# MLP up projection by quarter products in seven of eight iterations, with prepared activations fetched from memory in turn

## The chip, the cores and the metric

The kernel runs on one core of one Trainium2 chip. The metric is the device time of one execution in microseconds (us). The engines are named as in the profile: PE multiplies matrices (PEld is its weight load), DVE does elementwise work, ACT evaluates and copies, POOL issues part of the transfers, SP issues the others.

## The reference

One layer of a streaming encoder on x (1 x 1024 x 1024, f32): normalisation, three token-mixing branches, an output projection with a residual, and then the MLP, which is the part that is changed.

```python
x = x + rmsnorm(merged @ w_out[l], g_mix_post[l])
h = rmsnorm(x, g_mlp_pre[l])
f = jnp.square(jax.nn.relu(h @ w_up[l])) @ w_down[l]   # w_up 1024 x 4096, w_down 4096 x 1024
x = x + rmsnorm(f, g_mlp_post[l])
```

## The kernel before

Every f32 operand of a large product is held as a high part (hi: the value rounded by a copy on ACT) and a low part (lo: value minus hi, a subtraction on DVE). One product of a 128-deep slice is three matmuls of 128x512: hi by hi, hi by lo, lo by hi. `hThi`/`hTlo` hold the transposed MLP input h (8 slices k of 128 by 1024 tokens), `whi`/`wlo` and `raw` two slots (UP0, UP1) of 2048 columns of weights each, `yhi`/`ylo` the squared activations f, `acc` the output sum, and eight PSUM banks of 128x512, numbered by events n (bank n % 8), or taken as four pairs of 128x1024.

The MLP runs in eight iterations over 512 of the 4096 hidden units. In each, the up projection is eight pieces of 8 x 3 matmuls (192). The down projection of iterations 0 to 6 is already done by quarters: by the Strassen-Winograd scheme a 2 x 2 block product takes seven quarter products (`PRODUCTS`, 7 x 24 = 168 matmuls) instead of eight. DVE makes sums of quarters of f (`f_quad`) and differences of quarters of the weights (`w_diff`), ACT and DVE split them, and DVE adds finished pairs of banks to quarters of `acc` (`add_pair`, line 1621). The last iteration takes its down projection plainly (16 pieces of 12, 192 matmuls), because the final normalisation follows tile by tile.

Each engine works through a list written out by hand (in `mlp` of its block) and waits on semaphores. `w_hi`/`w_lo` count split weights, `f_sq`/`f_hi`/`f_lo` the activations, `pair_full`/`pair_free` the pairs of banks. SP loads a slot of `raw` (1 MB in two pieces of 512 KB) once the count of `w_lo` says that it has been read. A loop body covers iterations 1 to 6.

Of the kernel before, what the change touches and what calls it, by code (L numbers as in the profile page):

```python
# [16 lines left out]
P = 128  # L17
D = 1024
L = 1024
KT = D // P  # L20
NT = L // P
# [5 lines left out]
BT = W512 // P  # L27
# [95 lines left out]
PRODUCTS = [("A11", 0, 0), ("A12", 1, 1), ("S1", 2, 2), ("S2", 3, 3), ("S4", 0, 0), ("S3", 1, 2), ("A22", 2, 3)]  # L123


SET_A, SET_B = ("A11", "S2", "S3", "A22"), ("A12", "S1", "S4")
# [22 lines left out]
def hybrid_layer(nc, a, out):  # L149
# [4 lines left out]
    with ctx:  # L154
# [153 lines left out]
        sums_made, diffs_made, joined = sem("sums_made"), sem("diffs_made"), sem("joined")  # L308
        pair_full = [sem(f"pair_full{k}") for k in range(4)]
        pair_free = [sem(f"pair_free{k}") for k in range(4)]  # L310
        x1_back = [sem(f"x1_back{s}") for s in range(3)]
# [47 lines left out]
        W0 = U_MLP - U_QX  # L359
        UP0, UP1 = U_MLP % 2, 1 - U_MLP % 2  # L360
        RAW_D0, RAW_D1 = UP1, UP0
# [6 lines left out]
        def raw_half(slot, k):  # L368
# [3 lines left out]
        w_diff = {"T1": raw_half(RAW_D0, 0), "T2": raw_half(RAW_D0, 0), "B22": raw_half(RAW_D1, 1), "T3": raw_half(RAW_D1, 0),  # L372
                  "T4": raw_half(RAW_D0, 1)}
        w_place = {"T1": (UP1, 0), "T2": (UP1, 1), "B22": (UP0, 0), "T3": (UP1, 0), "T4": (UP1, 1)}
# [5 lines left out]
        def part_of(w, name):  # L380

            slot, k = w_place[name]
            return w[:, slot, 1024 * k:1024 * k + 1024]

        def pair_index(name, h):

            return h if name in SET_A else 2 + h

        def tiles_of(name):

            return (2, 3, 0, 1) if name == "A11" else range(4)

        def pair_count(name):

            return 1 + (SET_A if name in SET_A else SET_B).index(name)

        def pair_per(name):

            return 4 if name in SET_A else 3

        def wait_pair(eng, sems, name, h, it, done=0):

            count = pair_count(name) - 1 + done
            eng.wait_ge(sems[pair_index(name, h)], count + it * pair_per(name))

        def wait_pair_full(eng, name, h, it):
            wait_pair(eng, pair_full, name, h, it, 1)

        def f_place(s, c, h):

            return f_quad[("A11", "A12", "A21", "A22")[2 * h + s]][:, c, :]
# [7 lines left out]
        def _(sp):  # L419
# [65 lines left out]
            with sp.Fori(0, 8) as it:  # L485
                for s, count in ((0, W0 - 1), (1, W0)):
                    pieces = cols(U_MLP + s, up[:, bass.ds(it * 512 + s * 256, 256)])
                    sp.wait_ge(w_lo, count + it * 8)
                    for dst, src in pieces:
                        sp.dma_start(dst, src).then_inc(w_loaded[(U_MLP + s) % 2], 16)  # L490
                for s, slot, count in ((0, RAW_D0, W0 + 2), (1, RAW_D1, W0 + 1)):
                    pieces = cols(slot, down[bass.ds(it * 512, 512), s * 512:(s + 1) * 512], BT)
                    sp.wait_ge(w_lo, count + it * 8)
                    for dst, src in pieces:
                        sp.dma_start(dst, src).then_inc(w_loaded[slot], 16)
            rows = out[0].rearrange("(c i) d -> i c d", i=STEP)
            for t in range(NT):
                sp.wait_ge(out_made, t + 1)
                if t < NT - 1:
                    sp.dma_start(rows[t], tok[:, (1 + t % 3) * D:(2 + t % 3) * D]).then_inc(out_sent[t % 3], 16)  # L500
            c = (1 + (NT - 1) % 3) * D
            sp.dma_start(rows[NT - 1, :, 0:512], tok[:, c:c + 512]).then_inc(out_sent[1], 16)
            sp.wait_ge(out_made, NT + 1)
            sp.dma_start(rows[NT - 1, :, 512:D], tok[:, c + 512:c + D]).then_inc(out_sent[1], 16)
# [5 lines left out]
        def _(pool):  # L510
# [133 lines left out]
            pool.wait_ge(joined, 3)  # L644
            g.dma_start(tok[:, 0:D], a["g_mlp_post"][0].partition_broadcast(P)).then_inc(last_gain, 16)

            def x1_load(t):
                g.dma_start(tok[:, (1 + t % 3) * D:(2 + t % 3) * D], x1_dram[t * P:(t + 1) * P, :]).then_inc(x1_back[t % 3], 16)

            for t in range(3):  # L650
                x1_load(t)
# [6 lines left out]
        def _(act):  # L658
# [299 lines left out]
            def weight_hi(count, it, dst, source, load_of):  # L958

                act.wait_ge(*load_of)  # L960
                A.activation(dst, source, ACT.Copy).then_inc(w_hi, 1)  # L961

            def first_hi(it):
                wait_pair_full(act, "S4", 1, it)
                weight_hi(9, it, whi[:, UP0, :], raw[:, UP0, :], loaded(UP0, U_MLP, it + 1))

            def second_hi(it):
                wait_pair_full(act, "A22", 1, it - 1)
                weight_hi(2, it, whi[:, UP1, :], raw[:, UP1, :], loaded(UP1, U_MLP + 1, it))

            def third_hi(it):
                weight_hi(3, it, whi[:, UP0, :], raw[:, RAW_D0, :], loaded(RAW_D0, U_MLP + 3, it))

            def up_pieces(it, first):
                for pc, (s, c, h) in enumerate(UP_FIRST if first else UP_LATER):
                    n = up_event(pc, first)
                    if first and pc in (2, 3):
                        h2_hi(pc + 4)
                    if pc == (6 if first else 4):
                        wait_full(act, n - 1, it, 8)  # L980
                        third_hi(it)
                    if first and pc == 0:
                        act.wait_ge(sq_o, NT)
                        act.wait_ge(sq_x, NT)
                        act.wait_ge(x1_made, NT)
                    if first and pc == 2:
                        act.wait_ge(h2_made, NT)
                    if first and pc == 4:
                        act.wait_ge(x1_sent, 16 * NT)
                    wait_full(act, n, it, 8)  # L990
                    A.activation(f_place(s, c, h), banks[n % 8][:, :], ACT.Relu).then_inc(bank_free[n % 8], 1)  # L991
                    if h == 0:
                        act.wait_ge(f_sq, it * 8 + pc + 1)
                        A.activation(y_place(yhi, s)[:, c, :], f_place(s, c, h), ACT.Copy).then_inc(f_hi, 1)

            def f_hi_of(name, q, made, it):
                act.wait_ge(sums_made, it * 4 + made)
                A.activation(y_place(yhi, q), f_quad[name], ACT.Copy).then_inc(f_hi, 1)

            def w_hi_of(name, made, it):  # L1000
                if made:
                    act.wait_ge(diffs_made, it * 4 + made)
                A.activation(part_of(whi, name), w_diff[name], ACT.Copy).then_inc(w_hi, 1)

            def mlp(it, first):
                if not first:
                    second_hi(it)
# [1180 lines left out]
```

## Time and profile before

| what | us |
|---|---|
| median of 3 runs | 1515.39 (1513.56 to 1515.7) |
| profiled execution, its own time | 1513.69 |
| its span, first to last instruction | 1511.9 |
| PE busy | 1493.2 |
| DVE busy | 969.6 |
| ACT busy | 495.0 |
| POOL busy | 117.6 |

The span is that of one profiled execution; its own time lies 1.8 us above it. Busy time of PE counts overlapped matmuls once. A busy share says little by itself of what a change in one stage is worth; the chain that ended last does.

### The profile page before, as it was taken

The numbers are of one execution on the slowest core, as the hardware profiler recorded it, in microseconds if no ns is written. First come the engines' busy times: TensorE is split into PE (matmuls) and PEld (weight loads), VectorE is DVE, ScalarE is ACT, GpSimd is POOL, SyncE is SP. The second block draws the span as 40 slices with busy tenths as digits, with TensorE's granted clock in tenths as the row PEclk, the third lists the DMA queues.
The fourth block names the chain that finished last, engine by engine and source line by source line (L and its number), as shares of the span: only waits on it lengthen the run. The fifth ranks groups of instructions, "written<-read, shape, count | busy, mean of one in ns | idle before, by whom it ended". The sixth has DMA issues, their size and how long they took to land.

```text
span 1511.9 us, 18643 instructions
## 1 busy us (share of the span) xinstructions
PE 1493.2 (99%) x7366; PEld 1241.6 (82%) x7366; DVE 969.6 (64%) x1646; ACT 495.0 (33%) x670; POOL 117.6 (8%) x184
## 2 busy tenths in 40 slices
PE   8999999999999999999999999999999999999997
PEld 7888788888888888888888888888888888888886
DVE  6768568665844734446856776674839384856748
ACT  4435753322222352211334432222323232323232
POOL 0000000140220221000000200000000000000000
PEclk9999999999999999999999999999999999999999
DMA  8301121232112256324343303030211111020314
GB/s 320 71 28 56 63 78 38 102 112 105 64 64 100 61 165 205 104 86 152 131 126 106 98 1 111 0 112 0 67 44 55 55 55 55 28 83 1 110 56 181
DMA packets 82098, 130.44 MB, mean 86 GB/s; under 512 B 13128, under 2 KB 55152, under 8 KB 82032
## 3 DMA queue, kind: packets, MB, share of 16 engines
q1 hardware_dynamic: 67552, 80.23, 16.1%
q0 software_dynamic: 14480, 49.32, 9.6%
q8 instruction: 44, 0.72, 0.2%
q14 instruction: 22, 0.18, 0.0%
HBM read 104.36 MB, written 25.17 MB: 86 GB/s over the span
## 4 chain that ended last, share of the span: by engine, by line
PE 95%; DVE 4%; issue 0%; DMA 0%; ACT 0%; DVEq 0%; ACTq 0%; POOLq 0%
PE bank L1745 69%; PE bank L2140 18%; PE bank L1755 3%; PE bank L1785 1%; PE bank L1992 1%; PE bank L1878 1%; DVE tok L1714 1%; PE bank L2007 1%; PE bank L2012 1%; PE bank L1976 1%; PE bank L1893 0%; PE bank L1948 0%; DVE acc L1722 0%; DVE prob L1213 0%; DVE yst L1727 0%
## 5 line engine op out<-in xcount | busy, mean ns | idle before, releaser
L1745 PE MATMUL bank<-hThi,whi 128*128 128x512 f32 x1184 | 463.1, 391 | 0.5 <-DVE prob L1213 0.4
L1745 PE MATMUL bank<-hThi,wlo 128*128 128x512 f32 x1184 | 460.8, 389 | 0.0
L1745 PE MATMUL bank<-hTlo,whi 128*128 128x512 f32 x1184 | 460.8, 389 | 0.0
L1745 PEld LDWEIGHTS bank<-hThi,whi 128*128 128x128 f32 x1184 | 222.2, 188 | 47.9 <-issue 1.8
L1745 PEld LDWEIGHTS bank<-hThi,wlo 128*128 128x128 f32 x1184 | 222.3, 188 | 46.3
L1745 PEld LDWEIGHTS bank<-hTlo,whi 128*128 128x128 f32 x1184 | 222.3, 188 | 45.6
L2140 PE MATMUL bank<-whi,yhi 128*128 128x512 f32 x392 | 152.5, 389 | 0.0
L2140 PE MATMUL bank<-whi,ylo 128*128 128x512 f32 x392 | 152.5, 389 | 0.0
L2140 PE MATMUL bank<-wlo,yhi 128*128 128x512 f32 x392 | 152.5, 389 | 0.0
L1621 DVE TENSOR_TENSOR acc<-bank,acc 128x1024 f32<-128x1024 f32 x84 | 100.0, 1218 | 24.3 <-PE bank L2140 24.3
L1572 DVE TENSOR_TENSOR wlo<-raw,whi 128x1024 fp32r<-128x1024 f32 (+1 forms) x58 | 95.0, 1639 | 2.2 <-ACT whi L961 2.2
L345 ACT ACTIVATE whi<-raw 128x2048 fp32r<-128x2048 f32 x30 | 57.4, 1918 | 104.0 <-PE bank L1745 70.1
L351 DVE TENSOR_TENSOR wlo<-raw,whi 128x2048 fp32r<-128x2048 f32 x31 | 70.9, 2290 | 29.5 <-ACT whi L345 29.0
L2140 PEld LDWEIGHTS bank<-whi,ylo 128*128 128x128 f32 x392 | 73.6, 188 | 15.3
L2140 PEld LDWEIGHTS bank<-whi,yhi 128*128 128x128 f32 x392 | 73.6, 188 | 15.3
L2140 PEld LDWEIGHTS bank<-wlo,yhi 128*128 128x128 f32 x392 | 73.6, 188 | 15.3
L790 ACT ACTIVATE scr<-bank 128x512 f32<-128x512 f32 x48 | 28.5, 598 | 159.5 <-PE bank L1745 150.6
L1599 DVE TENSOR_TENSOR yst<-yst 128x512 f32<-128x512 f32 x28 | 19.4, 692 | 94.6 <-ACT yst L991 94.6
L961 ACT ACTIVATE whi<-raw 128x2048 fp32r<-128x2048 f32 x23 | 44.1, 1916 | 88.8 <-PE bank L2140 88.8
L1599 DVE TENSOR_TENSOR tok<-tok 128x512 f32<-128x512 f32 x28 | 19.3, 691 | 60.7 <-ACT tok L991 60.7
L991 ACT ACTIVATE yst<-bank 128x512 f32<-128x512 f32 x28 | 16.7, 598 | 115.7 <-PE bank L1745 115.7
L1448 DVE TENSOR_TENSOR tok<-bank,tok 128x512 f32<-128x512 f32 x8 | 5.5, 691 | 69.9 <-PE bank L2012 69.4
(361 smaller groups left out, 2192.3 us busy)
## 6 DMA issues: line engine op xcount, KB each, us to landing
raw<-in_w_in_dram SPq DMA_DIRECT2D x34, 512.0 KB, 4.6
raw<-in_w_up_dram SPq DMA_DIRECT2D x32, 512.0 KB, 4.3
raw<-in_w_down_dram SPq DMA_DIRECT2D x32, 512.0 KB, 5.1
gate_scratch<-scr POOLq DMA_DIRECT2D x48, 256.0 KB, 2.3
tok<-gate_scratch POOLq DMA_DIRECT2D x24, 512.0 KB, 3.6
y_scratch<-yst POOLq DMA_DIRECT2D x16, 256.0 KB, 2.5
yst<-y_scratch POOLq DMA_DIRECT2D x16, 256.0 KB, 4.1
raw<-in_w_out_dram SPq DMA_DIRECT2D x8, 512.0 KB, 4.3
```

Source lines behind the costliest of these rows:

```text
L345: nc.scalar.activation(parts(u)[0], raw[:, u % 2, :], ACT.Copy).then_inc(w_hi, 1)
L351: nc.vector.tensor_tensor(lo, raw[:, u % 2, :], hi.bitcast(f32), sub).then_inc(w_lo, 1)
L790: A.activation(scr[:, gp % 2, :], banks[n % 8][:, :], ACT.Sigmoid).then_inc(bank_free[n % 8], 1)
L961: A.activation(dst, source, ACT.Copy).then_inc(w_hi, 1)
L991: A.activation(f_place(s, c, h), banks[n % 8][:, :], ACT.Relu).then_inc(bank_free[n % 8], 1)
L1572: V.tensor_tensor(lo, source, hi.bitcast(f32), sub).then_inc(w_lo, 1)
L1599: V.tensor_tensor(f, f, f, mul).then_inc(f_sq, 1)
L1621: V.tensor_tensor(dst[:, 2 * h:2 * h + 2, :], psum[:, 2 * k:2 * k + 2, :], dst[:, 2 * h:2 * h + 2, :], add).then_inc(pair_free[k], 1)
L1714: V.scalar_tensor_tensor(out=xt[:, h], in0=yx[:, t % 2, h], scalar=y[:, k:k + 1], in1=xt[:, h], op0=mul, op1=add)\
L1745: ins = T.matmul(dst, lhs(k)[p], rhs(k)[q], start=start and k == 0 and i == 0, stop=stop and k == kt - 1 and i == 2)
L1755: ins = T.transpose(banks[n % 8][:, i * P:i * P + P] if dsts is None else dsts[i], src, by)
L2140: ins = T.matmul(banks[2 * k + t % 2][:, :], x[:, kk, rows], w[:, kk, :], start=opens and kk == 0 and i == 0, stop=kk == 1 and i == 2, ski ...
```

## The change

The up projection is done by seven quarter products as well, in iterations 1 to 7 (`up_phase(m)`, m = 0 to 6); the down projection stays at seven products in iterations 1 to 6 (`down_phase(m)`) and is plain in the first and in the last. The first iteration is plain in both parts (`plain_mlp`): 192 + 192 matmuls.

The up products need four combinations of quarters of h (T1 to T4). They are computed once, in the first iteration, by eight calls of `step(i)` on DVE (two halves of four sums), split by ACT (`step_high`) and DVE into the one buffer `staged` and stored by POOL to `h_scratch`; the plain quarter B11 is stored as well. T3 replaces a quarter of `hThi`/`hTlo` for good. T2 is fetched to the free half of `yhi`/`ylo` in each iteration; T1, T4 and B11 take turns in one quarter of `hThi`/`hTlo` (`turn_load`), fetched by POOL in two parts of 2 x 512 KB. A part is fetched when the half product that read it is done.

A repetition of the new loop body has on DVE 56 operations of 128x1024, on ACT 24, on PE 14 products of 24 matmuls: uP1, uP2, uP6, uP5, uP7, uP3, uP4, then dP1, dP5, dP6, dP3, dP7, dP2, dP4. There are 14 weight parts j = 0 to 13 (`W_PARTS`), each split by `w_hi_of(j)` and `w_lo_of(j)`.

```diff
+UP_PRODUCTS = [("uP1", 0, 0), ("uP2", 1, 1), ("uP6", 3, 2), ("uP5", 2, 3), ("uP7", 4, 0), ("uP3", 5, 1), ("uP4", 6, 2)]
+DOWN_PRODUCTS = [("dP1", 0, 1, 3), ("dP5", 2, 2, 0), ("dP6", 3, 3, 1), ("dP3", 0, 5, 2), ("dP7", 2, 6, 0), ("dP2", 1, 4, 1), ("dP4", 0, 7, 2)]
...
 SP
+            def mlp(m, last):
+                units = [down_unit(0, m + 1), down_unit(1, m + 1)]
+                if not last:
+                    units += [up_unit(0, m + 2), up_unit(1, m + 2)]
+                unit_load(UP0, units[0], w_count(5, m))
+                unit_load(UP1, units[1], w_count(6, m))
+                if not last:
+                    unit_load(UP1, units[3], w_count(11, m))
+                    unit_load(UP0, units[2], w_count(13, m))
...
 POOL
+            def turn_load(which, name, use, m):
+                pool.wait_ge(turn_used, use + 3 * m)
+                h_back(which, 0, turn, turn_in)
+                pair_ready(pool, name, m)
+                h_back(which, 1, turn, turn_in)
...
+            for i in range(8):
+                pool.wait_ge(step_lo, i + 1)
+                for hl in range(2):
+                    g.dma_start(h_dram[STEP_ORDER[i % 4], hl, :, 2 * (i // 4):2 * (i // 4) + 2, :], staged[hl]).then_inc(step_out, 16)
...
+            def streams(m, last):
+                turn_load(S_T1, "uP1", 1, m)
+                turn_load(S_T4, "uP5", 2, m)
+                if last:
+                    return
+                turn_load(S_B11, "uP4", 3, m)
+                pair_ready(pool, "dP2", m)
+                for k in range(2):
+                    h_back(S_T2, k, kept2, kept_in)
...
 ACT
+            def step_high(i):
+                act.wait_ge(step_made, i + 1)
+                if i:
+                    act.wait_ge(step_out, 32 * i)
+                A.activation(staged[0], step_sum(i), ACT.Copy).then_inc(step_hi, 1)
...
+                f_hi_of("A22", 0)
+                diff(8, m)
+                w_hi_of(13, m)
+                next_units(m + 1, [lambda: pair_ready(act, "dP7", m), lambda: pair_ready(act, "dP2", m), lambda: None])
...
 DVE
+            def step(i):
...
+                if i:
+                    dve.wait_ge(step_out, 32 * i)
+                dve.wait_ge(step_hi, i + 1)
+                V.tensor_tensor(staged[1], step_sum(i), staged[0].bitcast(f32), sub).then_inc(step_lo, 1)
...
+                    if pc == 6:
+                        prep_lo(dve, U_MLP + 2)
...
+                    if pc >= 4:
+                        step(pc - 4)
+                prep_lo(dve, U_MLP + 3)
+                for s in range(2):
+                    for t in range(NT):
...
+                        V.tensor_tensor(acc[:, t, h], banks[n % 8][:, :], acc[:, t, h], add).then_inc(bank_free[n % 8], 1)
+                        if t % 4 == 1:
+                            step(4 + 2 * s + t // 4)
+                        if s and t == 5:
+                            next_first(0)
+                for n in range(F + 16, F + 24):
+                    wait_taken(dve, n)
+                for k in range(4):
+                    dve.sem_inc(pair_free[k], 1)
...
+            def middle_quad(name, out_of, other, m):
+                pair_ready(dve, out_of, m)
+                k, q = pair_of(out_of, 1), f_quad[name]
+                V.tensor_tensor(q, pair_banks(k), f_quad[other], add).then_inc(pair_free[k], 1)
+                pair_read(dve, out_of, m)
+                V.scalar_tensor_tensor(out=q, in0=q, scalar=0.0, in1=q, op0=ALU.max, op1=mul).then_inc(f_sq, 1)
...
+                w_lo_of(6, m)
+                pair_read(dve, "uP6", m)
+                pair_read(dve, "uP5", m)
+                V.tensor_tensor(f_quad["A22"], f_quad["A22"], f_quad["A12"], add).then_inc(common_made, 1)
...
+                if last:
+                    join(2)
...
+                    dve.wait_ge(w_hi, w_count(7, m))
+                    V.tensor_tensor(wlo[:, UP0, :], raw[:, UP0, :], whi[:, UP0, :].bitcast(f32), sub).then_inc(w_lo, 1)
+                    middle_quad("A21", "uP3", "A12", m)
+                    f_lo_of("A21", 2, 3, m)
...
+                    return
+                w_lo_of(7, m)
+                dve.wait_ge(w_lo, w_count(7, m))
+                dve.wait_ge(*loaded(UP1, U_MLP + 3, m + 1))
+                w_diff(raw_half(UP0, 0), raw_half(UP1, 0), raw_half(UP0, 0), 5, m)
+                w_diff(raw_half(UP1, 0), raw_half(UP1, 1), raw_half(UP1, 0), 6, m)
+                dve.wait_ge(common_made, 1 + m)
+                middle_quad("A22", "uP7", "A22", m)
+                w_lo_of(8, m)
+                dve.wait_ge(w_lo, w_count(8, m))
+                w_diff(raw_half(UP0, 0), raw_half(UP1, 1), raw_half(UP0, 0), 7, m)
+                middle_quad("A21", "uP3", "A12", m)
+                w_lo_of(9, m)
+                squared(3, m)
+                dve.wait_ge(f_lo, 8 + 1 + 7 * m)
+                V.tensor_tensor(f_quad["S3"], f_quad["A11"], f_quad["A21"], sub).then_inc(sums_made, 1)
+                dve.wait_ge(sums_made, 1 + 4 * m)
+                V.tensor_tensor(f_quad["S1"], f_quad["A21"], f_quad["A22"], add).then_inc(sums_made, 1)
+                V.tensor_tensor(f_quad["S2"], f_quad["A22"], f_quad["S3"], sub).then_inc(sums_made, 1)
+                middle_quad("A12", "uP4", "A12", m)
+
+            def down_phase(m, first=False):
+                f_lo_of("S1", 2, 2, m)
...
+                f_lo_of("A22", 0, 7, m)
+                w_lo_of(13, m)
+                add_pair("dP7", 0, c22, m, "dP5")
+                add_pair("dP7", 1, c22, m, "dP5")
+                add_pair("dP2", 0, c11, m, "dP1")
+                w_lo_of(0, m + 1)
+                add_pair("dP2", 1, c11, m, "dP1")
+                dve.wait_ge(w_lo, w_count(0, m + 1))
+                dve.wait_ge(*loaded(UP1, U_MLP + 1, m + 2))
+                w_diff(raw_half(UP0, 0), raw_half(UP0, 0), raw_half(UP1, 0), 1, m + 1)
+                add_pair("dP4", 0, c21, m)
+                next_second(m + 1, lambda: add_pair("dP4", 1, c21, m))
...
 PE
-            mlp(0, True)
-            with pe.Fori(1, 7) as it:
-                mlp(it, False)
-            up_pieces(7, False)
+            plain_mlp()
+            with pe.Fori(0, 6) as m:
+                up_phase(m)
+                down_phase(m)
+            up_phase(6)
```

The last down projection and the final normalisation take the row tiles in the order 4 to 7, 0 to 3 (`tile_of`); the three sums of `common` into `acc` (2048 columns each) stand between DVE's operations of the last up phase.

## Rows read from the trace of the kernel before

**Rows 1.** The page: span, and busy time of the two busiest engines.

```profile
span 1511.9 us, 18643 instructions
...
PE 1493.2 (99%) x7366; PEld 1241.6 (82%) x7366; DVE 969.6 (64%) x1646; ACT 495.0 (33%) x670; POOL 117.6 (8%) x184
```

**Rows 2.** The chain that ended last, in order of time: start, us, what.

```profile
887.34 38.08 PE bank L2140 x168
...
1333.42 43.52 PE bank L1745 x192
1376.94 38.08 PE bank L2140 x168
1415.02 57.13 PE bank L1745 x252
1472.17 0.70 DVE acc L1722
```

**Rows 3.** Busy time by engine in one steady iteration: span, busy (count), clock, DMA.

```profile
1007.00:1089.00 82.00, 82.00 (x364) 67.89 (x363) 52.23 (x48) 23.28 (x26) 0.00 (x0) 1.00 0.15 51
```

**Rows 4.** Groups by line and shape in the MLP, 900 to 1490 us.

```profile
L1621 DVE TENSOR_TENSOR acc<-bank,acc 128x1024 f32<-128x1024 f32 x82 | 97.7, 1218 | 24.0 <-PE bank L2140 24.0
...
L1572 DVE TENSOR_TENSOR wlo<-raw,whi 128x2048 fp32r<-128x2048 f32 x22 | 50.2, 2282 | 2.2 <-ACT whi L961 2.2
L961 ACT ACTIVATE whi<-raw 128x2048 fp32r<-128x2048 f32 x22 | 42.1, 1916 | 88.8 <-PE bank L2140 88.8
L1572 DVE TENSOR_TENSOR wlo<-raw,whi 128x1024 fp32r<-128x1024 f32 x33 | 40.1, 1216 | 0.0
L1003 ACT ACTIVATE whi<-raw 128x1024 fp32r<-128x1024 f32 x32 | 33.1, 1054 | 35.3 <-DVE raw L1658 21.3 <-DVE raw L1638 14.0
...
L994 ACT ACTIVATE yhi<-tok 128x512 fp32r<-128x512 f32 x24 | 15.2, 633 | 18.2 <-DVE tok L1599 18.2
```

**Rows 5.** Timeline of DVE in a steady iteration: start, us, what, idle before.

```profile
1018.57 0.69 DVE L1599 TENSOR_TENSOR tok<-tok 128x512 f32<-128x512 f32 x1 [3.36 <-ACT tok L991]
1019.96 0.69 DVE L1603 TENSOR_TENSOR ylo<-tok,yhi 128x512 fp32r<-128x512 f32 x1 [0.70 <-ACT yhi L994]
...
1046.38 1.22 DVE L1613 TENSOR_TENSOR raw<-raw 128x1024 f32<-128x1024 f32 x1
1047.63 1.23 DVE L1615 TENSOR_TENSOR raw<-raw 128x1024 f32<-128x1024 f32 x1
...
1054.21 1.22 DVE L1572 TENSOR_TENSOR wlo<-raw,whi 128x1024 fp32r<-128x1024 f32 x1
1055.35 1.22 DVE L1588 TENSOR_TENSOR ylo<-yst,yhi 128x1024 fp32r<-128x1024 f32 x1
...
1069.48 1.22 DVE L1572 TENSOR_TENSOR wlo<-raw,whi 128x1024 fp32r<-128x1024 f32 x1
```

**Rows 6.** Timeline of SP: weight loads of one iteration, four pieces in each row.

```profile
1011.77 2.10 SPq L495 DMA_DIRECT2D raw<-in_w_down_dram  x4
1070.86 8.86 SPq L490 DMA_DIRECT2D raw<-in_w_up_dram  x4
```

**Rows 7.** Landing of `raw` pieces issued 1070 to 1073, 1012.4 to 1014, 845 to 860 us.

```profile
DMA to landing us min/median/max: 3.6/4.0/4.4
...
DMA to landing us min/median/max: 4.4/5.6/6.3
...
DMA to landing us min/median/max: 7.9/7.9/7.9
```

**Rows 8.** Landing of single 512 KB stores by POOL, issued at 773.8 and 847.3 us.

```profile
x_scratch<-yst POOLq DMA_DIRECT2D x1, 512.0 KB, 2.9
...
x_scratch<-yst POOLq DMA_DIRECT2D x1, 512.0 KB, 6.6
```

**Rows 9.** Landing of one load in the crowded first 60 us of the kernel.

```profile
vT<-in_w_mem_kv_dram SPq DMA_DIRECT2D x1, 512.0 KB, 10.6
```

**Rows 10.** Timeline of ACT: fifth up piece of the first iteration.

```profile
871.12 0.60 ACT L991 ACTIVATE yst<-bank 128x512 f32<-128x512 f32 x1 [3.51 <-PE bank L1745]
```

More of the change, by code:

```diff
@@ L385, in pair_index @@
[L385 to L404, printed above, removed]
@@ new lines, in plain_mlp @@
+                for i, (t, s) in enumerate((t, s) for s in range(2) for t in range(NT)):
+                    n = F + 8 + i
+                    if t == 0:
+                        unit(U_MLP + 2 + s)
+                    hi, lo = wviews(U_MLP + 2 + s, BT)
+                    wait_free(pe, n)
+                    if s == 0 and t in (0, 4):
+                        pe.wait_ge(f_lo, 6 if t == 0 else 8)
+                    product(banks[n % 8][:, :], yT(slice(t * P, t * P + P)), lambda k: (hi[:, k, :], lo[:, k, :]), BT)\
+                        .then_inc(bank_full[n % 8], 1)
@@ new lines, in up_phase @@
+            def up_phase(m):
+                turn, kept3 = ([h_quarter(y, 0, t) for y in (hThi, hTlo)] for t in range(2))
+                b21, b22 = ([h_quarter(y, 1, t) for y in (hThi, hTlo)] for t in range(2))
+                kept2 = [second_half(y) for y in (yhi, ylo)]
+                moving = {"uP1": turn, "uP2": b21, "uP6": kept2, "uP5": turn, "uP7": kept3, "uP3": b22, "uP4": turn}
+                for name, j, place in UP_PRODUCTS:
+                    k = pair_of(name, 1)
+                    pe.wait_ge(w_lo, w_count(j, m))
+                    pe.wait_ge(pair_free[k], pair_before(k, name, m))
+                    hi, lo = (w_slot(w, place).rearrange("p (k c) -> p k c", k=4) for w in (whi, wlo))
+                    h, opens = moving[name], name not in ("uP6", "uP3", "uP4")
+                    use = ("uP1", "uP5", "uP4").index(name) if h is turn else None
+                    for part in range(2):
+                        if h is turn:
+                            pe.wait_ge(turn_in[part], 32 * (1 + use) + 96 * m)
+                        if h is kept2:
+                            pe.wait_ge(kept_in[part], 32 + 32 * m)
+                        for c in range(2):
+                            for kk in (2 * part, 2 * part + 1):
+                                for i, (w, x) in enumerate(((hi, h[0]), (hi, h[1]), (lo, h[0]))):
+                                    ins = T.matmul(banks[2 * k + c][:, :], w[:, kk, c * P:c * P + P], x[:, kk, :], start=opens and kk == 0 and i == 0,
+                                                   stop=kk == 3 and i == 2, skip_group_check=True)
+                        if part:
+                            ins.then_inc(pair_full[k], 1)
+                        elif h is turn:
+                            ins.then_inc(turn_used, 1)
```

563 lines of the change are left out of this document (327 added, 236 removed).

## The prediction

> **What bounds the kernel now.** I read the page first: PE is busy for 1493.2 of 1511.9 us, DVE for 969.6 [rows 1]. A busy share is no proof, so the chain that ended last came next. Through the MLP it holds only PE: up projections of 43.52 us for 192 matmuls and down projections of 38.08 us for 168 follow each other without a gap, and the last 252 matmuls take 57.13 us. All give 0.2267 us a matmul [rows 2]. DVE enters the chain only at 1472.17 us, for the final normalisation. Then the stretch of one steady iteration (81.6 us, read over 82): PE is busy throughout at a granted clock of 1.00 (the 2.4 GHz level), DVE for 52.2 us, ACT for 23.3, the DMA engines for 0.15 of it [rows 3]. So taking matmuls away is worth their whole time until another queue is late.
>
> The profiled execution took 1513.69 us by its own time, 1.7 below the median of the runs; I subtract from 1513.69 and add 1.7 at the end.
>
> **Matmuls.** Before: 7 x (192 + 168) + 192 + 192 = 2904 of 512 columns. After: 384 in the first iteration, 6 x 336, and 168 + 192 in the last, 2760. So 144 go: 144 x 0.2267 = 32.6 us. They have the shape of the others. A product is 24 matmuls, 5.44 us; a repetition of the loop is 76.16 us if PE never waits.
>
> **Prices of the walk.** I walk through the lists. DVE: an operation of 1024 columns lasts 1.22 us [rows 4], the next one starts 1.13 after it, or 1.25 if it waits for its result [rows 5]. The new operation (maximum and product in one) is not in these rows; between 1.13 and the 1.25 of a dependent one, I take 1.25, as it does depend. ACT: 1.05 us for 1024 columns, 1.92 for 2048 [rows 4]. A handover between engines is about 0.03 us: DVE idles 0.70 around a copy of 0.633 [rows 4, 5]. A weight slot has landed 5.1 us after the `w_lo` that releases it: that operation ends at 1070.70, SP issues at 1070.86 and 0.57 later, the second piece lands 4.4 us on [rows 5 to 7].
>
> **DVE is nearly full.** 56 operations of 1.13 us are 63.5 of 76.16 us, and some wait. With t = 0 where uP1 starts, the products end at 5.44, 10.88, 16.32 (uP6), 21.76 (uP5), 27.20 (uP7), 32.64 (uP3), 38.08 (uP4), and each down product 5.44 later. Up to uP5 DVE waits for PE (its operation on uP2 starts at 10.93). Then:
> - ACT takes uP5's banks, 21.8 to 22.84. DVE: common sum 22.87, w_lo 7 at 24.0, w_diff 5 at 25.25 at best, since it waits for w_lo 7 and for a weight slot.
> - w_diff 6 26.5, two operations on uP7 27.6 and 28.9, w_lo 8 30.0, w_diff 7 31.3, and then uP3, ready at 32.69: a slack of 0.3.
> - From there nine operations back to back (uP3 twice, w_lo 9, S3, S1, S2, uP4 twice, f_lo S1) end at 43.34. dP5 starts at 43.52 and needs S1: a slack of 0.15.
> - In the down phase 20 operations run to w_lo 13, which ends at 65.1. That releases slot UP0, landed at 70.2; ACT's w_hi 0, w_lo 0 at 71.3, the add of dP2, w_diff 1, the first add of dP4, which ends at 75.95. It frees the pair that uP1 needs at 76.16: a slack of 0.2.
> - The split of weights for uP2 ends 2.1 us into the next repetition, for uP6 at 8.4, each ahead of use.
>
> PE is therefore kept busy by a chain of DVE with about 0.4 us of slack over 54 us. What makes w_diff 5 late makes dP5 late, and every repetition longer.
>
> **The fetch that is late.** w_diff 5 needs slot UP1, released by w_lo 6 at 19.61. Alone it lands at 24.7, in time. But POOL starts on T4 at 19.04 (half of uP5 is done): two pieces at once, two more at 21.76. Four pieces issued within 2.1 us have all landed 1.7 + 6.3 = 8.0 us after the first issue [rows 6, 7]: 19.1 + 8.0 = 27.1. A store that joins four loads 2.5 us later moves the last load from 6.3 to 7.9 us [rows 7] and itself takes 6.6 instead of 2.9 [rows 8], so the two pieces at 21.76 can add 1.6: 28.7. I take 27.5, nearer the first, since of the four pieces the slot's two were issued last but share the engines with the other queue. Its cost: 27.53 - 25.25 - 0.42 of slack = 1.8 us a repetition, 10.8 in six. Bounds: 0, if the slot lands as alone, and 5.3 (31.6 in all), if its second piece takes the 10.6 us of the crowded start [rows 9] from 20.3 on.
>
> The Trainium skill (DMA: Bandwidth & Descriptors, Anatomy of one DMA) fits a transfer as 2.0 us plus its bytes at 436 GB/s. For the four pieces (2.1 MB) that is an estimate of 6.8 us against the 8.0 of the row; the slot would be there at 25.9 and the cost 0.3 a repetition, 1.6 in all. The row decides. The same page (Queues, rings and completion order) says that a DMA engine takes the queues that have work in turn, which would let T4 halve the slot's rate; no row separates this.
>
> The other fetches of a repetition are costed at nothing. T1 has from 2.7 and 5.4 to 16.3; T4 is issued by 22.3 and needed from 32.6; B11 and T2 are issued 40 and 16 us ahead. They would cost what they are late. 12.6 MB in 76 us are 165 GB/s, where 51 take a share of 0.15 [rows 3], so the engines are half used. ACT's 24 operations (25 us) hide as long as none is last in a handover; where one is, it stands in the walk.
>
> **The first iteration** gets its 24 matmuls more (counted), and DVE 26 more operations: eight steps of three or four. `staged` is one buffer, so lo of a step comes after the stores of the step before: handover, two stores, ACT's hi, DVE's lo. Two stores together are not shown; one alone lands in 2.9 us, one beside four loads in 6.6 [rows 8], a pair of loads in 5.1; I take 5.1. From the fifth piece, whose copy starts at 871.12 [rows 10]: lo of step 0 ends at 879.7, stores landed 884.8, hi and lo of step 1 end at 887.15. ACT starts on the first down weights behind that hi, at 885.8, DVE splits them at 887.8, done 890.1, where PE is ready at 887.34 [rows 2]: 2.8 us idle. Behind DVE now queue adds to `acc` and PE's banks. The steps go on at 7.4 to 10 us each (lo ends at 896.8, 904.3, 914.3, 921.7, 929.2, 937.2). PE's 16 down tiles (2.72 us each, 43.5) end at 933.7, but uP1 waits for the last add, behind step 7, w_lo 0 and w_diff 1: 940.9. 7.2 us idle. With stores of 2.9 this falls to about 7.5 in all, with 6.6 it is 17.5.
>
> **The last iteration.** DVE splits 2048 columns of w_down only when uP3 has released them (ACT 32.7 to 34.6, DVE to 36.9), then takes uP3 (38.1, 39.3), ACT's hi to 40.4, lo to 41.7. The plain down projection needs that quarter at 38.08: 3.6 us idle. Of two bounds (0 by PE, 3.6 by the walk) I take the walk. The final part is the same work behind PE; its start moves with PE, and the adds that wait (DVE is free 5.7 us after the down start) are caught up before 13.6, where its chain begins.
>
> **Sum.** 32.6 - 2.8 - 7.2 - 3.6 - 10.8 = 8.2 us. 1513.69 - 8.2 = 1505.5; on the scale of the runs 1507.2.
>
> **Rivals.**
> - The slot is hidden: T4's first pieces are ahead and the slot lands by 25.7. 19.0 us gained, 1496.4. For: the engines are used at 0.15 now, and POOL's 0.7 us lead. Against: [rows 7, 8] show five pieces slowing each other. Chance 0.25.
> - Slower: the loads meet as in the first 60 us, the slot lands at 30.9, 5.3 us a repetition: 19.0 - 31.6 = -12.6, 1528.0. It decides from 3.2 us a repetition, a landing at 28.9. Against: the five pieces of [rows 7, 8] have none above 7.9. Chance 0.13.
> - The stores cost 6.6 us: the first iteration idles 17.5 instead of 10, gain 0.7, 1514.7, no change. For: some of the eight pairs meet weight loads and the fetch of T3. Against: most are alone. Chance 0.12.
> - The forecast, stores near 5 us and a stall of 0.5 to 2.6 at dP5: 0.45, its own range 1502 to 1514. The rest, 0.05, is an order that I walked wrongly.
>
> A run of this kernel tells about 0.2% (3.0 us) from no change: 1512.4 to 1518.4. Faster: 0.45 + 0.25 and 0.02 of the others, 0.72; same 0.12; slower 0.16. The range reaches from the hidden slot (1496) to part of the slower case: 1495 to 1520.
>
> **What would show it.** The stretch of a repetition: 76.2 us (hidden), 78 (forecast), over 79.4 (slower); DVE busy about 64 of it; PE idle at dP5 with DVE's f_lo of S1 as releaser, and DVE idle ahead of w_diff 5 with a DMA into `raw`. PE idle 2.8 us ahead of the first down tile, 7 ahead of uP1, 3.6 ahead of the last down part. Idle at uP5 or uP4 itself would mean that the turned quarters are late, and idle at uP1 that slot UP0 is; both would make the prediction wrong by a place that I price at nothing.

## The result, and the profile after

The changed kernel takes 1528.44 us (median of 4, 1525.75 to 1530.46), the kernel before 1515.4 in the same comparison: ratio 1.0087, 95% interval 1.0070 to 1.0105. It is slower by 13 us. The forecast was 1507.2 with a range up to 1520, so the sign and the range were both wrong. Its own forecast for a single profiled execution was 1505.5; that execution took 1530.46, 25.0 us more. These 25.0 us are what has to be explained.

The page of the changed kernel, its span and the busy time of the engines:

```profile
span 1528.7 us, 18594 instructions
...
PE 1478.7 (97%) x7222; PEld 1224.8 (80%) x7222; DVE 1072.6 (70%) x1721; ACT 507.2 (33%) x663; POOL 202.1 (13%) x314
```

Beside [rows 1]: 144 matmuls fewer, as planned, but PE's busy time fell by only 14.5 us where 144 matmuls are 32.6. The rest of those 32.6 came back as busy time, which points to slower matmuls; the windows below show where. DVE has 103 us more.

The chain that ended last, in order of time (start, duration, what), for the first iteration, one repetition of the loop that starts at 1110.31, the two after it, and the last iteration:

```profile
924.74 5.38 DMA h_scratch<-tok
...
933.44 6.13 DMA h_scratch<-tok
...
945.95 18.99 PE bank L2372 x72
...
1110.31 16.33 PE bank L2372 x72
...
1128.67 1.24 DVE wlo L1768
...
1130.33 7.93 DMA raw<-in_w_down_dram
1138.37 1.24 DVE raw L1778
...
1155.11 1.23 DVE ylo L1772
1156.55 35.78 PE bank L2392 x144
1192.33 16.34 PE bank L2372 x72
...
1238.56 32.94 PE bank L2392 x144
1271.51 16.34 PE bank L2372 x72
...
1431.67 32.65 PE bank L2372 x144
...
1473.53 15.35 PE bank L1968 x60
```

Where [rows 2] had nothing but PE, the chain now leaves PE in every repetition, after the first half of the up phase: a split of weights on DVE (1128.67), the load of a down weight slot (7.93 us), `w_diff 5` (1138.37), DVE's list up to the low part of S1 (1155.11), and then PE's down phase. Two more things are to be read here. The 144 matmuls behind `dP5` take 35.78 us in one repetition and 32.94 in another: the same instructions, so the clock differs. And uP1 of the first repetition begins at 945.95, behind stores of the prepared sums.

PE's waits from 860 to 1480 us (place, what ended them: sum, count, longest, in us):

```profile
PE bank L2392 <- DVE ylo L1772: 16.6, 6, 3.0
...
PE bank L2372 <- DVEq L1761: 8.6, 1, 8.6
...
PE bank L1968 <- DVE ylo L1772: 3.8, 1, 3.8
PE bank L1968 <- DVE wlo L364: 2.2, 1, 2.2
```

They are the four places of the forecast, in the order of these lines: dP5 in each of six repetitions (2.77 us each, forecast 1.8), uP1 of the loop (8.6, forecast 7.2), the last down part (3.8, forecast 3.6), the first down tile (2.2, forecast 2.8). Their sum is 31.2 where the forecast had 24.4. That explains 6.8 us of 25.0.

The windows of three repetitions, and of 2 us steps behind the idle time of the second, then the first 4 us of the loop and the first 6 us of the last down part (stretch, length, busy of PE, PEld, DVE, ACT, POOL, granted clock, DMA share, GB/s):

```profile
1029.70:1110.30 80.60, 78.08 (x337) 64.12 (x337) 65.49 (x57) 24.52 (x25) 10.61 (x16) 0.98 0.52 156
1110.30:1192.30 82.00, 79.28 (x338) 65.03 (x337) 65.55 (x57) 24.62 (x25) 10.60 (x16) 0.96 0.50 153
1192.30:1271.50 79.20, 76.48 (x338) 63.00 (x337) 64.40 (x56) 24.22 (x24) 10.59 (x16) 1.00 0.52 160
...
1154.30:1156.30 2.00, 0.00 (x0) 0.00 (x0) 2.00 (x3) 1.59 (x2) 0.00 (x0) 0.87 0.06 18
1156.30:1158.30 2.00, 1.75 (x4) 1.47 (x5) 2.00 (x3) 0.00 (x0) 0.00 (x0) 0.50 0.00 0
1158.30:1160.30 2.00, 2.00 (x6) 1.52 (x6) 2.00 (x3) 0.00 (x0) 0.00 (x0) 0.50 0.00 0
1160.30:1162.30 2.00, 2.00 (x7) 1.52 (x6) 2.00 (x3) 0.00 (x0) 0.00 (x0) 0.50 0.00 0
1162.30:1164.30 2.00, 2.00 (x10) 1.62 (x9) 2.00 (x3) 1.07 (x1) 0.00 (x0) 0.92 0.00 0
...
946.00:950.00 4.00, 4.00 (x10) 3.13 (x11) 3.69 (x4) 1.06 (x1) 3.40 (x5) 0.50 0.08 19
...
1474.00:1480.00 6.00, 6.00 (x22) 4.74 (x22) 5.93 (x6) 1.31 (x2) 0.53 (x1) 0.78 0.01 3
```

Beside [rows 3]: the clock column is no longer 1.00 throughout. Behind the idle time that ends at 1156.55 the granted clock stands at 0.50 (the 1.2 GHz level) for 6 us, with PE busy in every one of them. A repetition of 79.2 us kept its clock; the others paid for it. DVE is busy for 64.4 to 65.5 us, where the forecast said about 64.

The slot that is late: landing of the `raw` pieces issued from 1110 to 1133 us (against [rows 7]), and DVE's timeline in the same repetition:

```profile
DMA to landing us min/median/max: 3.8/4.6/7.9
```

```profile
1134.38 1.22 DVE L1768 TENSOR_TENSOR wlo<-raw,whi 128x1024 fp32r<-128x1024 f32 x1
1138.37 1.23 DVE L1778 TENSOR_TENSOR raw<-raw 128x1024 f32<-128x1024 f32 x1 [2.77 <-DMA raw<-in_w_down_dram]
```

DVE stands still for 2.77 us ahead of `w_diff 5` for a piece that needs 7.9 us. The window of that landing shows what the share of 0.50 for the whole repetition hides:

```profile
1129.90:1138.30 8.40, 8.40 (x39) 6.96 (x38) 2.36 (x2) 1.98 (x2) 2.58 (x4) 1.00 0.93 283
```

The DMA engines are 0.93 busy while the slot is on its way (0.60 in the 5.2 us in which the same slot lands when T4 is held back). The prediction's "the engines are half used" was an average over 76 us. Placed on the forecast's own clock (t = 0 at uP1, 1110.31): w_lo 6 ends at 19.59 (forecast 19.61), the slot has landed at 27.96 (forecast 27.5), w_diff 5 starts at 28.06 (27.53), dP5 at 46.24 where 43.52 would be without a wait.

### The profile page after: what moved, and what is told of

It is laid out like the page before. It is cut to its first block, busy times and chain, and to the rows that moved or that the text cites. A ratio compares the mean times of both kernels' runs of the same rounds, so it can differ in the third digit from the quotient of the medians.

```text
span 1528.7 us, 18594 instructions
## 1 busy us (share of the span) xinstructions
PE 1478.7 (97%) x7222; PEld 1224.8 (80%) x7222; DVE 1072.6 (70%) x1721; ACT 507.2 (33%) x663; POOL 202.1 (13%) x314
## 4 chain that ended last, share of the span: by engine, by line
PE 78%; DVE 11%; DMA 5%; issue 4%; ACT 2%; POOL 0%; DVEq 0%; SPq 0%; ACTq 0%; POOLq 0%
PE bank L1968 47%; PE bank L2392 13%; PE bank L2372 9%; DMA raw<-in_w_down_dram 3%; PE bank L1978 3%; PE bank L2008 2%; DMA h_scratch<-tok 1%; DVE wlo L1768 1%; DVE yst L1809 1%; PE bank L2215 1%; PE bank L2101 1%; DVE tok L1936 1%; DVE raw L1778 1%; DVE ylo L1772 1%; PE bank L2230 1%
## 5 line engine op out<-in xcount | busy, mean ns | idle before, releaser
L1968 PE MATMUL bank<-hThi,whi 128*128 128x512 f32 x736 | 288.8, 392 | 0.5 <-DVE prob L1350 0.4
L1968 PE MATMUL bank<-hThi,wlo 128*128 128x512 f32 x736 | 286.5, 389 | 0.0
L1968 PE MATMUL bank<-hTlo,whi 128*128 128x512 f32 x736 | 286.5, 389 | 0.0
L1079 ACT ACTIVATE whi<-raw 128x1024 fp32r<-128x1024 f32 x91 | 95.9, 1056 | 207.1 <-DVE raw L1778 119.8
L1968 PEld LDWEIGHTS bank<-hThi,whi 128*128 128x128 f32 x736 | 138.2, 188 | 30.5 <-issue 1.8
L1968 PEld LDWEIGHTS bank<-hThi,wlo 128*128 128x128 f32 x736 | 138.1, 188 | 28.9
L1968 PEld LDWEIGHTS bank<-hTlo,whi 128*128 128x128 f32 x736 | 138.2, 188 | 28.1
L2392 PE MATMUL bank<-whi,yhi 128*128 128x512 f32 x336 | 134.5, 400 | 16.6 <-DVE ylo L1772 16.6
L2372 PE MATMUL bank<-hThi,whi 128*128 128x512 f32 x336 | 131.8, 392 | 8.6 <-DVEq L1761 8.6
L2372 PE MATMUL bank<-hTlo,whi 128*128 128x512 f32 x336 | 131.7, 392 | 0.0
L2372 PE MATMUL bank<-hThi,wlo 128*128 128x512 f32 x336 | 131.5, 391 | 0.0
L1768 DVE TENSOR_TENSOR wlo<-raw,whi 128x1024 fp32r<-128x1024 f32 x91 | 110.9, 1219 | 29.2 <-ACT whi L1079 29.1
L358 ACT ACTIVATE whi<-raw 128x2048 fp32r<-128x2048 f32 x32 | 61.2, 1916 | 104.2 <-PE bank L1968 70.2
L2392 PEld LDWEIGHTS bank<-whi,yhi 128*128 128x128 f32 x336 | 64.9, 193 | 32.9 <-issue 19.1
L2372 PEld LDWEIGHTS bank<-hThi,whi 128*128 128x128 f32 x336 | 63.7, 190 | 22.3 <-issue 9.0
L1778 DVE TENSOR_TENSOR raw<-raw 128x1024 f32<-128x1024 f32 x52 | 63.6, 1222 | 20.0 <-DMA raw<-in_w_down_dram 16.9
```

Of the source, the lines that this page charges most:

```text
L358: nc.scalar.activation(parts(u)[0], raw[:, u % 2, :], ACT.Copy).then_inc(w_hi, 1)
L1079: A.activation(w_slot(whi, place), source, ACT.Copy).then_inc(w_hi, 1)
L1768: V.tensor_tensor(w_slot(wlo, place), source, w_slot(whi, place).bitcast(f32), sub).then_inc(w_lo, 1)
L1778: V.tensor_tensor(dst, x, y, sub if count != 2 else add).then_inc(diffs_made, 1)
L1968: ins = T.matmul(dst, lhs(k)[p], rhs(k)[q], start=start and k == 0 and i == 0, stop=stop and k == kt - 1 and i == 2)
L2372: ins = T.matmul(banks[2 * k + c][:, :], w[:, kk, c * P:c * P + P], x[:, kk, :], start=opens and kk == 0 and i == 0, stop=kk == 3 and i == ...
```

## Where the 25.0 us are

| place | forecast | measured | difference |
|---|---|---|---|
| all up to 870 us, unchanged code | 0 | later by 2.4 | 2.4 |
| first iteration, up to uP1 of the loop | uP1 at 940.9 | 943.6 (945.95 less the 2.4) | 2.7 |
| loop: idle ahead of dP5, six times | 10.8 | 16.6 | 5.8 |
| loop: low clock behind idle time | 0 | 10.4 | 10.4 |
| loop: small pauses | 0 | 0.3 a repetition | 1.8 |
| last iteration, 1431.67 to the end | 95.0 | 97.0 | 2.0 |

The differences add up to 25.1; the rest is rounding. The clock's 10.4 are read from equal pieces of work: the six groups of 144 matmuls take 34.56, 34.57, 35.78, 32.94, 32.95 and 34.54 us, 7.7 more than six times 32.94; the first 72 matmuls of the loop take 18.99 instead of 16.33, 2.7 more.

The first line is not the change's doing. One group of 16 matmuls of the memory projection starts at about the same time in both executions and takes longer in one. The chain of the kernel before and, under it, of the changed one:

```profile
10.87 3.69 PE bank L1785 x16
```

```profile
10.92 6.06 PE bank L2008 x16
```

Everything up to 870 us is shifted by those 2.4 us. Between 12 and 14 us PE does 6 matmuls in the second and 11 in the first, though the clock column shows 1.00 in both; why is open. The group takes 3.69 us in eight of the profiled executions of this record, 6.06 in two and 5.36 in one, so two medians that lie some 2 us apart can differ by this alone.

## The experiments

All of them start from the changed kernel. Those with a filler add matmuls that nothing reads; nothing is left out in any. Two readings of the loop stood against each other. One: POOL's fetch of T4 is ahead of the weight slot in the DMA engines, this makes `w_diff 5` and so dP5 late, and the low clock is what follows from PE's pause. The other: DVE's list is too full, or the slot is slow by itself, and the clock falls for a reason of its own.

**T4 behind the slot.** POOL waits until slot UP1 has landed before it fetches T4.

```diff
+                pool.wait_ge(*loaded(UP1, U_MLP + 3, m + 1))
                 turn_load(S_T4, "uP5", 2, m)
```

> POOL starts the fetch of T4 only when the weight slot that w_diff 5 waits for has landed. Theory (the two loads meet on the DMA engines, the slot lands 8.3 us after its release instead of 5.1, PE idles about 3 us at dP5 and the granted clock then falls for some us): no idle at dP5 beyond 0.3 us, a repetition takes 76.2 to 76.8 us instead of 80.95 on average, and the time is 1528.4 - 6 x 4.45 = 1501.7 us (1499 to 1505). Rival (DVE's 56 operations and their handovers are too long by themselves, the slot is only the last of several): a repetition stays at 79 us or more and the time above 1518.

Measured: 1506.68 us (1502.64 to 1507.6), ratio 0.9949 (0.9932 to 0.9966), against 1515.13 for the kernel before. It is 21.8 us less than the changed kernel, and faster than the kernel before. The median is 1.7 us above the expected interval; the profiled execution (1502.64) is the fastest of the four. Landing of the slot pieces of a repetition, the chain for a repetition, its window, PE's waits and DVE's timeline around `w_diff 5`:

```profile
DMA to landing us min/median/max: 3.6/4.1/4.7
```

```profile
1022.20 38.08 PE bank L2373 x168
...
1065.89 32.95 PE bank L2393 x144
```

```profile
1022.20:1098.80 76.60, 76.42 (x337) 62.95 (x337) 64.94 (x57) 24.36 (x24) 10.59 (x16) 1.00 0.55 164
```

```profile
PE bank L2373 <- DVEq L1762: 8.6, 1, 8.6
...
PE bank L2393 <- DVE ylo L1773: 0.7, 4, 0.2
```

```profile
1122.91 1.22 DVE L1769 TENSOR_TENSOR wlo<-raw,whi 128x1024 fp32r<-128x1024 f32 x1
1124.36 2.49 DVE L1779 TENSOR_TENSOR raw<-raw 128x1024 f32<-128x1024 f32 x2 [0.24 <-DVE wlo L1769]
```

The last piece needs 4.7 us instead of 7.9, DVE's pause of 2.77 is gone, PE waits 0.7 us at dP5 in four repetitions together, the clock is 1.00, and the repetition takes 76.6 us, where 76.16 is what its matmuls need. DVE's busy time is the same, 64.9 us: the list was not too full. T4 itself, fetched later, is waited for once, 0.4 us in the last iteration. One wait on POOL takes away the idle time and the low clock of the loop together: it takes 462.2 us (943.18 to 1405.37) instead of 485.7. The pause ahead of the last down part is 3.1 us long here, and the clock stays at 1.00 behind it.

**A filler in PE's pause.** Twelve matmuls that nothing reads fill most of the pause ahead of dP5. The pause stays, so the difference is the clock alone.

```diff
             def down_phase(m):
                 for p, (name, q, parts_made, place) in enumerate(DOWN_PRODUCTS):
+                    if name == "dP5":
+                        pe.wait_ge(pair_free[2], pair_before(2, name, m))
+                        filler(banks[4], 12)   # matmul(banks[4], hThi[:, 4, 512:640], hThi[:, 4, 512:1024])
                     pe.wait_ge(f_lo,
```

> PE runs 12 matmuls of 128x512 whose result nobody reads (2.7 us, into a bank that dP5 opens anew) ahead of its wait at dP5; everything else is as changed. Theory (half the loss over the wait itself is the clock that falls after the idle time): the granted clock stays at 1.00 and all six repetitions take 79.0 to 79.5 us, as the two that kept their clock; 1528.4 - 6 x 1.75 = 1518 us (1515 to 1521). Rival (the low clock has another cause, or the filler delays dP5): 1526 or more.

Measured: 1521.43 us (1519.34 to 1522.82), ratio 1.0045 (1.0029 to 1.0062). The chain of one repetition and its window:

```profile
1104.91 38.08 PE bank L2372 x168
...
1151.28 32.89 PE bank L2399 x144
```

```profile
1104.90:1184.20 79.30, 79.17 (x350) 65.28 (x349) 65.13 (x57) 24.36 (x24) 10.60 (x16) 1.00 0.52 158
```

The clock stays at 1.00 at dP5. Five repetitions take 79.0 to 79.3 us, where the changed kernel had 79.2 to 82.0; the first still takes 82.0 (83.7), since the low clock at uP1 isn't touched by this edit, and there "all six" was a miss. DVE's lateness is untouched. The loop takes 477.8 us instead of 485.7, the median is 7.0 lower: that was the clock behind the pauses at dP5, and it goes with the pauses. The clock has no reason of its own. The time is 0.4 us above the expected interval; the length of a repetition is as expected.

**Order in the last iteration.** DVE takes uP3's products ahead of the split of 2048 columns of weights.

```diff
+                    middle_quad("A21", "uP3", "A12", m)
                     dve.wait_ge(w_hi, w_count(7, m))
                     V.tensor_tensor(wlo[:, UP0, :], raw[:, UP0, :], whi[:, UP0, :].bitcast(f32), sub).then_inc(w_lo, 1)
-                    middle_quad("A21", "uP3", "A12", m)
```

> In the last up phase DVE takes uP3's pair before it splits the 2048 columns of w_down. Theory (the last down projection waits 3.8 us for the low part of that quarter, and then runs some us at the low clock): its start moves 3.2 us earlier and the clock stays, 1528.4 - 4.6 = 1524 us (1522.5 to 1526). Rival (the final DVE chain sets the end, so an earlier start of PE is lost in it): 1527.5 or more.

Measured: 1522.17 us (1520.84 to 1522.59), ratio 1.0050 (1.0033 to 1.0067), 6.3 us less than the changed kernel. PE's wait ahead of the last down part is down from 3.8 us to 0.6. The place was read rightly. The median is 0.3 us below the expected interval, and part of the 6.3 us isn't this edit's: in its profiled execution the untouched loop takes 483.2 us instead of 485.7, since fewer repetitions fell to the low clock.

**Only T4's second half behind the slot.** POOL's two first pieces go as in the changed kernel, and the two others wait. This asks which pieces hold the slot up.

```diff
                 h_back(which, 0, turn, turn_in)
                 pair_ready(pool, name, m)
+                if name == "uP5":
+                    pool.wait_ge(*loaded(UP1, U_MLP + 3, m + 1))
                 h_back(which, 1, turn, turn_in)
```

> Only the second half of T4 waits until the weight slot has landed; the first half still starts with it. Theory A (the two pieces issued later take engine time from the slot, the term that the prediction halved): the slot lands at 27.1 us of a repetition or before instead of 27.96, w_diff 5 starts 0.9 us or more earlier, a repetition takes 77.8 to 78.4 us where the clock stays at 1.00 (79.2 as changed), time 1519 to 1523. Theory B (only what is queued ahead of the slot delays it): landing at 27.9 and no change, 1527 to 1530.

Measured: 1523.07 us (1519.72 to 1524.19), ratio 1.0063 (1.0045 to 1.0081). The time alone would speak for a gain of 5.4 us. The rows don't: landing of the slot's pieces in the repetition that starts at 1105.03, DVE's timeline there, and PE's waits:

```profile
DMA to landing us min/median/max: 3.7/4.6/7.8
```

```profile
1132.99 2.48 DVE L1780 TENSOR_TENSOR raw<-raw 128x1024 f32<-128x1024 f32 x2 [2.67 <-DMA raw<-in_w_down_dram]
```

```profile
PE bank L2394 <- DVE ylo L1774: 14.9, 6, 2.6
```

The last piece lands after 7.8 us, not 7.9; `w_diff 5` starts at 1132.99 - 1105.03 = 27.96 of the repetition, not 28.06; the wait at dP5 is 2.5 us, not 2.8. This is the slowest of the six: in their mean DVE idles 2.5 us ahead of `w_diff 5`, where it is 2.8 in the changed kernel and 0.2 with all of T4 behind the slot. So it is T4's first two pieces that delay it (in the changed kernel's repetition at 1110.31 they are issued at 1129.67 and 1130.36, the slot's last piece at 1130.33), and the two issued 2.4 and 3.1 us after the slot's last piece cost 0.3 us a repetition. Of the 5.4 us, 1.7 are those waits. The rest is covered by the clock, which fell in two repetitions of this execution and in four of the other (34.52, 32.93, 34.54, 32.95, 32.95, 32.93 us for 144 matmuls: 3.2 us instead of 7.7). Which repetitions fall isn't set by the code alone.

**Order at the end of the first iteration.** Step 7 of the preparation moves behind the last adds and the weights for the loop, on DVE and ACT; POOL fetches T2 and T1 for the first repetition ahead of the last two stores.

```diff
 DVE
-                        if t % 4 == 1:
+                        if t % 4 == 1 and not (s and t == 5):
                             step(4 + 2 * s + t // 4)
...
                 next_second(0)
+                step(7)
 POOL
-            for i in range(8):
+            for i in range(7):
                 sum_out(i)
...
+            pool.wait_ge(step_out, 32 * 7)
+            turn_load(S_T1, "uP1", 1, 0)
+            sum_out(7)
```

> In the first iteration the last of the eight sums is made, split and stored after the last adds into acc and after the first weight splits of the loop, and the fetches of T2 and T1 go ahead of its stores. Theory (the steps' wait for stores holds the adds that free PE's banks): PE idles 1 to 3 us ahead of uP1 instead of 8.6, uP1 starts some 5 us earlier, and the low clock behind it shrinks; 1528.4 - 6 = 1522.5 us (1520 to 1525). Rival (the delay only moves into uP6 or uP5, whose operands come later): 1527 or more, with PE idle at one of these.

Measured: 1518.21 us (median of 9, 1516.88 to 1526.44), ratio 1.0031 (1.0016 to 1.0046), 10.2 us less. PE's waits at uP1 (the first line) and at uP6 (the second), and a window behind uP1's start:

```profile
PE bank L2382 <- DVEq L1770: 1.5, 1, 1.5
PE bank L2382 <- DVE wlo L1778: 1.2, 1, 1.2
```

```profile
940.00:946.00 6.00, 6.00 (x28) 4.98 (x27) 4.76 (x5) 1.06 (x1) 3.47 (x6) 1.00 1.14 379
```

2.7 us of waiting instead of 8.6, and no low clock behind it (2.7 us more). These are 8.6 of the 10.2 us. The median is 1.8 us below the expected interval; a part of the delay, 1.2 us, did move to uP6, as the rival said. What held uP1 was step 7, with its wait for the stores of step 6, ahead of the last adds. A kernel that stores only a quarter of each sum, meant to tell the stores from DVE's own operations, gave no result, so what the stores cost by themselves is not shown.

**Two orders together.** The edits "T4 behind the slot" and "order in the last iteration".

> T4 after the slot, and in the last up phase uP3's pair before the weight split. If the two losses lie in different stretches and add: 1506.7 - 6 = 1501 us (1499 to 1503). If one hides the other: 1505 or more.

Measured: 1501.73 us (1499.78 to 1502.2), ratio 0.9915 (0.9897 to 0.9933). The gain over "T4 behind the slot" is 5.0 us, where the second edit alone gave 6.3: they add, but for 1.3 us.

**All orders.** The three edits, and the split of the first slot of down weights moved from piece 6 to piece 5 of the plain up projection, ahead of step 1, for the wait of 2.2 us at the first down tile.

```diff
+                    if pc == 5:
+                        prep_lo(dve, U_MLP + 2)
-                    if pc == 6:
-                        prep_lo(dve, U_MLP + 2)
                     if pc >= 4:
                         step(pc - 4)
```

> As e7, and the first iteration with its last sum at the end, and with the split of the first w_down slot ahead of the second sum (ACT and DVE, at the sixth up piece). Theory: no idle time ahead of the first down tile (2.2 us as changed), at most 3 ahead of uP1 (8.6), clock near 1.00 in the whole MLP: 1501 - 8 to 10 = 1492 us (1489 to 1496), against 1482.8 for 144 matmuls fewer and nothing lost. Rival (the same work is only late at another place): above 1498.

Measured: 1493.29 us (1492.82 to 1493.83), ratio 0.9863 (0.9846 to 0.9881). That is 20.5 us less than the kernel before in this comparison (1513.74) and 35.2 less than the changed kernel. One part missed: the wait at uP1 is 5.2 us, where at most 3 were expected, and a low clock follows it. PE reaches the loop earlier now, while DVE's adds and splits ahead of it take as long as before.

**A filler ahead of the loop, beside the same kernel without it.** Twenty unread matmuls between the plain part and the loop, and the kernel "all orders" once more in the same comparison.

```diff
             plain_mlp()
+            wait_taken(pe, F + 16)
+            for _ in range(20):
+                T.matmul(banks[1][:, :], hThi[:, 4, 512:640], hThi[:, 4, 512:1024], start=True, stop=True, skip_group_check=True)
             with pe.Fori(0, 6) as m:
```

> As e8, with 20 matmuls of 128x512 (4.5 us) that nobody reads in the 5.2 us in which PE there waits for its banks ahead of uP1. Theory of the clock: the granted clock stays at 1.00 from 937 us on instead of 0.50 and 0.84 over the first 6 us, which cost e8 about 2.0 us; 1493.3 - 2.0 = 1491.3 us (1490.3 to 1492.3). Rival (the filler itself delays uP1, or the low clock does not come from the idle time): 1493 or more.

> e8 once more, beside e9 on the same chip, for the difference between the two: 1493.3 us (1492.3 to 1494.3).

Measured: 1493.18 us (1492.72 to 1495.03), ratio 0.9860 (0.9844 to 0.9877), with the filler; 1495.58 (1494.97 to 1495.86), ratio 0.9873 (0.9856 to 0.9889), without. The windows around the loop's start, without the filler and with it:

```profile
939.00:942.00 3.00, 3.00 (x8) 2.32 (x8) 3.00 (x3) 1.06 (x1) 0.00 (x0) 0.50 1.10 325
942.00:945.00 3.00, 3.00 (x14) 2.46 (x13) 2.83 (x3) 0.10 (x1) 1.01 (x2) 0.91 1.02 374
```

```profile
937.00:940.00 3.00, 3.00 (x13) 2.49 (x14) 2.82 (x3) 1.06 (x1) 0.00 (x0) 1.00 1.15 339
940.00:943.00 3.00, 3.00 (x15) 2.46 (x15) 2.97 (x3) 0.00 (x0) 1.43 (x3) 1.00 1.06 376
```

At 0.50 three us hold 8 matmuls, at 1.00 they hold 13: the filler keeps the clock, and it doesn't delay uP1 (936.95, against 936.81 in the first comparison of "all orders"). But the difference of 2.4 us between the medians, close to the 2.0 expected, is not its worth. The 16 early matmuls that no edit touches, in the chain without the filler and, under it, with it, and a wait of PE with the filler:

```profile
10.74 5.36 PE bank L2019 x16
```

```profile
10.69 3.69 PE bank L2019 x16
```

```profile
PE bank L2383 <- DVE wlo L1779: 1.2, 1, 1.2
```

In the profiled executions the spans differ by 2.3 us, and 1.7 of them are these matmuls. From uP1 to the second repetition the kernel takes 78.4 us with the filler and 79.0 without: 0.6 us gained, where the low clock had cost 2.1 (72 matmuls in 18.41 us instead of 16.33). PE now reaches uP6 before its weights are split and waits 1.2 us there for DVE. So the low clock ahead of the loop hid a wait, and most of its cost can't be had back by the clock alone. The time itself, 1493.18, lies above the interval (1490.3 to 1492.3) and where the rival had it.

The same 16 matmuls tell why the kernel without the filler took 1495.58 here and 1493.29 in the comparison before: 5.36 us in this profiled execution, 3.69 in that one, and spans of 1493.2 and 1491.6. For the executions without a profile this is not shown. "All orders" is 1493 to 1496 us, some 1.3% faster than the kernel before.

## Why the prediction was wrong, step by step

- **Matmuls (right).** 144 fewer, 0.2267 us each wherever the clock is 1.00: 24 x 7 = 168 take 38.08 us as in [rows 2].
- **"PE is therefore kept busy by a chain of DVE with about 0.4 us of slack" (right, with less slack).** The walk through DVE's list gave w_lo 6 to 0.02 us. The slack was about 0.1 us: with the slot in time, `w_diff 5` starts at 25.52 instead of 25.25, since operations that wait for a result or a count start some 0.1 us later than priced.
- **"The fetch that is late" (place and cause right, size wrong: 1.8 us a repetition, measured 2.77).** The landing was 0.5 us later than taken, and the slack 0.3 less: 5.8 us in six. The experiment with T4 behind the slot shows the cause. The bound of 1.6 us for "the two pieces at 21.76" was the wrong piece of the sum: those two add 0.3; the slot's second piece pays for T4's first two. The row of four pieces (8.0 us) was the nearest guide: the four here have landed 8.6 us after the first issue.
- **The step that failed: a pause of PE was priced as its own length.** The sum takes 2.8, 7.2, 3.6 and 6 x 1.8 us off and nothing for what PE does afterwards. In fact the granted clock fell to 0.50 behind the 8.6 us, behind four of the six pauses at dP5, and in part (0.78 over 6 us) behind the 3.8. In the loop this is 10.4 us, in the last iteration about 1.4, nearly half of the 25.0. Without these 11.8 the median would be about 1516.6, an estimate: inside the range, and no change. The filler at dP5 shows it: same lateness, no low clock, 7.9 us less in the loop. The one ahead of the loop shows the limit: of 2.1 us it gives back 0.6, because DVE is next. The clock of 1.00 in [rows 3] was read as a property of the kernel, where it was one of a PE without pauses. The Trainium skill (TensorE: Matmul & The Clock Gate, Part 1) says that the throttled state is the default and that activity releases it. The traces agree, at 0.50 behind four of the six pauses and 1.00 behind the fillers; two pauses of 2.7 and 2.8 us kept 1.00. The prediction did not weigh this rule.
- **First iteration (right in kind, 2.7 us too low).** The waits were 2.2 and 8.6 us for 2.8 and 7.2. Most pairs of stores had landed 3.7 us after the second issue, a little faster than priced, but the last ones, beside the fetch of T3, took 5.4 and 6.1; and behind the 2.2 us pause the clock was 0.80 over the 6 us from 894 to 900.
- **Last iteration (3.6 forecast, 3.8 measured).** Shown by its experiment.
- **At nothing:** the turned quarters T1 and T4, B11, and slot UP0. PE waited for none of them in the loop.
- **The rivals.** "Slower" named 1528.0, which is what came. It is no hit: it had the slot at 30.9 and 5.3 us of idle a repetition, and the runs show 28.0 and 2.77, with the clock for the rest. Its stated threshold ("it decides from 3.2 us a repetition") was passed: 2.77 of idle, 1.7 of clock (10.4 over six) and 0.3 of small pauses are 4.8, which is why the sign turned. "The slot is hidden" is the kernel with T4 behind the slot, whose repetition of 76.6 us is close to the 76.2 named for it.
- **Run to run.** 2.4 us of this execution lie in code that the change doesn't touch; the median of the runs is 2.0 below it.

Open: why two pieces on POOL's queue, issued 0.66 us before the slot's last piece and together with it, hold that piece back by 3.2 us (7.9 against 4.7), while two issued 2.4 us later cost 0.3. The Trainium skill (DMA: Bandwidth & Descriptors, Queues, rings and completion order) has the engines take the queues in turn, which by itself would make later pieces cost as well; the experiment with the second half later shows 0.3 us for it. No run took this apart further.

## What to carry to other kernels

Price a new pause of the matrix engine as the pause plus what the slower clock costs behind it: read the granted clock in the windows right behind existing pauses, and don't take 1.00 from a stretch that has none. Take off what the next wait would have cost anyway. Read the DMA share in the stretch in which the transfer is under way, not over the whole iteration. Where a fetch with much slack and one with none are issued within a microsecond of each other, make the one with slack wait for the other: here a single wait on an idle queue was worth 21.8 us. Judge a small edit by the rows of its place, since times of whole runs also move with which pauses happen to drop the clock, and with stretches that the edit doesn't touch.

## What the runs showed of the hardware that was not expected

- Pauses of 2.5 to 3.0 us between stretches of full activity dropped the granted clock to 0.50 in four of six repetitions, not in all; it then stayed there for 3.4 to 6 us of busy PE, which cost 1.6 to 2.8 us. A pause of 2.2 us was followed by 0.80 over 6 us.
- The length of the pause didn't decide it: in order, 3.02, 2.52 and 2.72 us fell, 2.72 and 2.79 didn't, 2.85 fell; and 3.1 us ahead of the last down part (T4 behind the slot) kept 1.00.
- Twelve unread matmuls on an otherwise waiting PE kept the clock at 1.00 through a pause of the same kind.
- Two 512 KB pieces on one queue, issued within 0.7 us of it, moved the last piece of another queue's load from 4.7 to 7.9 us, with the DMA engines 0.93 busy in that stretch and 0.50 over the repetition.
